# Routed experts on one core: rows without a token skipped, results scattered by GpSimd, spare wide places given to narrow pieces, two preplaced experts

## What the reference computes

```
p_top, g_sel = lax.top_k(p_group, 1)                      # one of 4 groups
e_val, e_sel = lax.top_k(fine, TOP_E)                     # two of its 8 experts
gate = (p_top * jax.nn.softmax(e_val, axis=-1)).reshape(-1)
...
def expert_block(args):
    xb, e = args
    return (jax.nn.silu(xb @ w_gate[e]) * (xb @ w_up[e])) @ w_down[e]
...
out = jnp.zeros((n_tok + 1, d), y_rows.dtype).at[row_token].add(y_rows)[:n_tok]
```

```
layer 0: 21 24 57 58 18 4 1 21 | 1 0 0 0 0 1 0 2 | 25 21 1 22 14 14 28 13 | 96 64 79 163 11 205 0 60
layer 1: 2 82 6 32 15 8 24 9 | 88 35 12 38 24 39 1 47 | 54 193 21 7 48 170 35 28 | 1 0 0 2 1 0 2 0
```

## Time and profile before

| | |
|---|---|
| median of the runs before | 3147.11 us (3146.6 to 3148.13, 3 runs) |
| the profiled execution's own time | 3154.01 us |
| its span in the profile | 3152.0 us |
| TensorE busy | 2810.8 us (89% of the span) |
| VectorE / ScalarE / GpSimd busy | 1619.1 / 679.5 / 410.1 us |
| moved by DMA | 685.03 MB, mean 217 GB/s |

### The profile page before, as it was taken

How to read it: one execution, slowest core, us unless ns; L and a number is a source line. 1 busy time by engine, 2 the same in 40 slices (tenths; PEclk the granted TensorE clock), 3 DMA queues, 4 the chain that set the end, 5 groups by cost and what they waited for, 6 DMA issues and landing times. The chain is left out here.

```text
span 3152.0 us, 36064 instructions
## 1 busy us (share of the span) xinstructions
PE 2810.8 (89%) x13430; PEld 1853.9 (59%) x13430; DVE 1619.1 (51%) x2277; ACT 679.5 (22%) x1202; POOL 410.1 (13%) x257
## 2 busy tenths in 40 slices
PE   9988999999989999969978999785989969999884
PEld 7777888877777887736763333334766743333331
DVE  5575898565567996576971111114667651111112
ACT  1242111022323110073230000003336220000001
POOL 0010113211101113200000000001324000000000
PEclk9998999999989999989989999988999979999897
DMA  5132765233324663164249999995213279999997
GB/s 186 54 141 82 240 207 167 107 120 99 121 93 148 214 218 108 63 185 127 67 157 374 394 392 393 395 405 181 80 53 124 77 264 385 394 391 393 400 395 297
DMA packets 251498, 685.03 MB, mean 217 GB/s; under 512 B 23600, under 2 KB 140316, under 8 KB 197068
## 3 DMA queue, kind: packets, MB, share of 16 engines
q1 hardware_dynamic: 243436, 656.15, 56.7%
q0 software_dynamic: 7904, 26.74, 2.7%
HBM read 628.78 MB, written 54.05 MB: 217 GB/s over the span
## 5 line engine op out<-in xcount | busy, mean ns | idle before, releaser
L2824 PE MATMUL bank<-expert_w_raw,expert_x_turned 128*64 128x512 f32 x2240 | 552.2, 641 | 99.3 <-DMA expert_w_raw<-in_moe_w_up_dram 49.3
L2824 PEld LDWEIGHTS bank<-expert_w_raw,expert_x_turned 128*64 128x64 f32 x2240 | 168.1, 147 | 420.7 <-issue 383.0
L153 PE MATMUL bank<-first_XH,first_w_high 128*128 128x512 f32 (+1 forms) x944 | 370.2, 392 | 0.1
L154 PE MATMUL bank<-first_XL,first_w_high 128*128 128x512 f32 (+1 forms) x944 | 363.4, 385 | 0.0
L155 PE MATMUL bank<-first_XH,first_w_low 128*128 128x512 f32 (+1 forms) x944 | 363.2, 385 | 0.0
L2916 DVE TENSOR_TENSOR expert_hidden<-expert_silu,bank 64x512 f32<-64x512 f32 x70 | 47.5, 679 | 588.0 <-ACT expert_silu L2892 588.0
L233 DVE TENSOR_TENSOR first_w_low<-first_w_raw,first_w_high 128x2048 fp32r<-128x2048 f32 (+2 forms) x94 | 287.1, 3054 | 3.2
L2850 PE MATMUL bank<-expert_w_raw,expert_hidden_turned 128*64 128x512 f32 x1120 | 253.5, 597 | 0.9 <-ACT expert_hidden_turned L2886 0.9
L2775 POOL DMA_INDIRECT expert_x_rows<-h_rows,slot_token x70 | 65.8, 940 | 1126.5 <-PE bank L2800 852.3
L153 PEld LDWEIGHTS bank<-first_XH,first_w_high 128*128 128x128 f32 x944 | 179.7, 190 | 43.9 <-issue 9.8
L154 PEld LDWEIGHTS bank<-first_XL,first_w_high 128*128 128x128 f32 x944 | 179.8, 191 | 37.1 <-issue 2.9
(11 more groups left out here) (550 smaller groups left out, 4665.9 us busy)
## 6 DMA issues: line engine op xcount, KB each, us to landing
expert_w_raw<-in_moe_w_gate_dram SPq DMA_DIRECT2D x120, 1024.0 KB, 17.9
expert_w_raw<-in_moe_w_up_dram SPq DMA_DIRECT2D x120, 1024.0 KB, 20.1
expert_w_raw<-in_moe_w_down_dram SPq DMA_DIRECT2D x120, 1024.0 KB, 20.5
ffn_mod_w<-in_ada_w_dram SPq DMA_DIRECT2D x48, 1024.0 KB, 4.9
first_w_raw<-in_w_up_dram SPq DMA_DIRECT2D x88, 512.0 KB, 6.3
first_w_raw<-in_w_down_dram SPq DMA_DIRECT2D x22, 1024.0 KB, 4.8
first_w_raw<-in_w_in_dram SPq DMA_DIRECT2D x20, 1024.0 KB, 5.0
y_rows<-expert_y SPq DMA_DIRECT2D x140, 128.0 KB, 16.7
```

What stands on the lines that cost most here:

```text
L153: nc.tensor.matmul(out, rounded(st[0]), rounded(mv[0]), start=start, stop=False)
L154: nc.tensor.matmul(out, rounded(st[0]), rounded(mv[1]), start=False, stop=False)
L2824: last = nc.tensor.matmul(out, xT[:, h.parity, kk, :], weights.view(s.parity, 2 * part + w)[:, k, :], start=(kk == 0), stop=(kk == KD - 1))
```

## The change

- `FIRST_EXPERTS` is (0, 16) and no longer 0, 1, 2; each wide place is followed by three narrow ones (`APART` 4); the loop has 15 turns and no longer 17.
- A wide place that no expert needs takes a narrow piece (`at_narrow`, `past_wide`). With the counts above the pattern now makes 28 spans with 33 halves in layer 0 and 30 spans with 35 halves in layer 1, 58 spans and 68 halves in all.
- An empty slot gets an index out of bounds, and the gather skips it; its rows in SBUF keep what they held, so they are zeroed once per phase.
- The result of a half is laid out as 64 rows of 1024 (two products of 64x512 instead of one of 128x512), and GpSimd scatters its rows with an indirect DMA, which skips empty slots too (`slot_row`). SyncE stores nothing any more. The store of span n-2 stands on GpSimd between the gathers of n and of n+1; the last two halves are scattered by `tail_row`.

```diff
-FIRST, WIDE = 3, 5
-NARROW = EXPERTS + (SEQ * TOP_E - EXPERTS) // HALF + 1
+FIRST_EXPERTS, WIDE, APART = (0, 16), 5, 4
+FIRST = len(FIRST_EXPERTS)
+LEAD = WIDE * (APART - 1)
+FIXED = FIRST + WIDE + LEAD
+FURTHER = (EXPERTS + (SEQ * TOP_E - EXPERTS) // HALF + 1 - LEAD) // 2 - 1
+NARROW = LEAD + 2 * FURTHER + 2
...
-LEAD = 2 * WIDE + 2
-FIXED = FIRST + WIDE + LEAD
-FURTHER = (NARROW - LEAD) // 2 - 1
...
+TAIL = 2
+NOWHERE = 16384
...
-        link(V.scalar_tensor_tensor(self.gap, self.narrow_at[:, 0:E], float(HALF), self.gap, ALU.mult, ALU.add))
+        link(V.tensor_scalar(self.at_narrow, self.narrow_at[:, 0:E], self.wide_at[:, E:E + 1], float(WIDE), ALU.add, ALU.subtract))
+        link(V.scalar_tensor_tensor(self.at_narrow, self.at_narrow, 0.0, self.at_narrow, ALU.min, ALU.add))
+        link(V.scalar_tensor_tensor(self.gap, self.at_narrow, float(HALF), self.gap, ALU.mult, ALU.add))
...
-        link(V.tensor_scalar(self.token[0:HALF, :], self.LIST[0:HALF, 0:HALVES], 1.0, 0.0, ALU.subtract, ALU.max))
-        V.tensor_copy(G["slot_token"][0:HALF, :], self.token[0:HALF, :]).then_inc(self.slots_ready, 1)
...
+        link(V.tensor_scalar(self.empty[low, :], listed, 0.5, float(NOWHERE), ALU.is_lt, ALU.mult))
+        link(V.scalar_tensor_tensor(self.token[low, :], self.empty[low, :], -1.0, listed, ALU.add, ALU.add))
+        V.tensor_copy(G["slot_token"][low, :], self.token[low, :]).then_inc(self.slots_ready, 1)
+        push(V.tensor_tensor(self.place_of[low, :], self.empty[low, :], c2["half_row"][low, :], ALU.add))
...
-            def store(s, done=None):
-                for h in s.halves:
-                    sp.wait_ge(y_done, h.at(1))
-                    for c in range(2):
-                        sp.dma_start(G["y_dram"][bass.ds(h.first_row(), HALF), c * BANK:(c + 1) * BANK], y[HALF * c:HALF * c + HALF, h.parity, :]
-                                     ).then_inc(done or stored[h.parity], 16)
...
-                    store(Span(n - 3, j))
...
+            def gather(n):
+                for h in Span(n).halves:
+                    if h.n >= 2:
+                        pool.wait_ge(rows_turned, h.n - 1)
+                    pool.indirect_dma_start(xg[h.parity][:, :], None, G["h_dram"][:, :],
+                                            bass.IndirectOffsetOnAxis(ap=G["slot_token"][0:HALF, h.row:h.row + 1], axis=0),
+                                            bounds_check=SEQ - 1, oob_is_err=False).then_inc(rows_loaded[h.parity], 16)
+
+            def scatter(h, at, done):
+                return pool.indirect_dma_start(G["y_dram"][:, :], bass.IndirectOffsetOnAxis(ap=at, axis=0), y[:, h.parity, :], None,
+                                               bounds_check=BLOCKS * P - 1, oob_is_err=False).then_inc(done, 16)
+
+            def store(n):
+                for h in Span(n).halves:
+                    pool.wait_ge(y_done, 2 * (h.n + 1))
+                    scatter(h, G["slot_row"][0:HALF, h.row:h.row + 1], stored[h.parity])
...
+            for s in range(2):
+                nc.gpsimd.memset(xg[s][:, :], 0.0).then_inc(rows_zeroed, 1)
...
             for n in range(FIXED + 2):
-                for h in Span(n).halves:
-                    gather(h)
+                if n == FIRST:
+                    pool.wait_ge(chain.table_set, 1)
+                gather(n)
+                if n >= TAIL:
+                    store(n - TAIL)
...
-                            dve.wait_ge(stored[h.parity], h.turns(32))
-                        nc.vector.tensor_tensor(y[:, h.parity, :], down_bank(h)[:, :], gain[:, :], ALU.mult).then_inc(y_done, 1)
+                            dve.wait_ge(stored[h.parity], h.turns(16))
+                        for c in range(2):
+                            at = slice(HALF * c, HALF * (c + 1))
+                            nc.vector.tensor_tensor(y[:, h.parity, c * BANK:(c + 1) * BANK], down_bank(h)[at, :], gain[at, :], ALU.mult
+                                                    ).then_inc(last_y_done if last or end else y_done, 1)
```

More of the change, by code:

```diff
@@ L1695, in constant_parts_2 @@
     along = lambda a: np.broadcast_to(np.asarray(a, np.float32), (P, len(a)))
-    own = np.where(np.arange(EXPERTS) < FIRST, HALF, 0)
-    origin = np.where(np.arange(EXPERTS) < FIRST, HALF * np.arange(EXPERTS), 0)
+    own, origin = np.zeros(EXPERTS), np.zeros(EXPERTS)
+    for n, e in enumerate(FIRST_EXPERTS):
+        own[e], origin[e] = HALF, HALF * n
     parts["first_rows"] = along(own)
@@ L2403, in __init__ @@
         self.idx = [now(TT, 1) for _ in range(2)]
-        self.rest, self.n_wide, self.wide_end, self.wide, self.gap_wide, self.second, self.gap, self.n_narrow = [now(EXPERTS) for _ in range(8)]
+        self.rest, self.n_wide, self.wide_end, self.wide, self.gap_wide, self.second, self.gap, self.n_narrow, self.at_narrow, self.ends_narrow = [now(EXPERTS) for _ in range(10)]
         self.wide_at, self.narrow_at = [now(EXPERTS + 1) for _ in range(2)]
@@ L2589, in __init__ @@
         self.parity = n % 2
-        k, place = divmod(n - FIRST, 3)
-        self.wide = FIRST <= n < FIRST + 3 * WIDE and place == 0
+        k, place = divmod(n - FIRST, APART)
+        self.wide = FIRST <= n < FIRST + APART * WIDE and place == 0
         wides = min(max(0, k + (place > 0)), WIDE)
@@ L2762, in _ @@
             for r in range(UP, PLACES):
-                weights.load(sp, r, 1, 1)
-            more = walk(sp, further(sp), step)
-            for n in (FIXED, FIXED + 1):
-                store(Span(n, more), last_stored)
-            sp.wait_ge(last_stored, 64)
+                weights.load(sp, r, 1, second)
+            walk(sp, further(sp), step)
         @block.gpsimd
         def _(pool):
-            def gather(h):
-                if h.n >= 2:
-                    pool.wait_ge(rows_turned, h.n - 1)
-                pool.indirect_dma_start(xg[h.parity][:, :], None, G["h_dram"][:, :],
-                                        bass.IndirectOffsetOnAxis(ap=G["slot_token"][0:HALF, h.row:h.row + 1], axis=0)
-                                        ).then_inc(rows_loaded[h.parity], 16)
@@ L2788, in _ @@
                     for odd in range(2):
-                        gather(Span(FIXED + 2 * pair + odd).halves[0])
+                        gather(FIXED + 2 * pair + odd)
+                        store(FIXED + 2 * pair + odd - TAIL)
+            pool.wait_ge(tail_set, 1)
+            for q in range(TAIL):
+                pool.wait_ge(last_y_done, 2 * (q + 1))
+                scatter(Span(FIXED + q).halves[0], G["tail_row"][0:HALF, q:q + 1], last_stored)
+            pool.wait_ge(last_stored, 32)
         @block.tensor
@@ L2936, in _, with read @@
             dve.wait_ge(gain_set, 2)
-            walk(dve, further(dve), step)
+            def read():
+                more = further(dve)()
+                nc.vector.tensor_copy(G["tail_row"][0:HALF, :], G["slot_row"][0:HALF, bass.ds(Span(FIXED + 2 - TAIL, more).halves[0].at(), TAIL)]
+                                      ).then_inc(tail_set, 1)
+                return more
+            walk(dve, read, step)
 class Combine:
```

61 lines of the change are left out of this document (39 added, 22 removed).

## The result

The changed kernel takes **3294.5 us** (median of 4 runs, 3285.5 to 3303.0) where the kernel before takes 3146.9 beside it (4 runs, 3144.3 to 3148.1): ratio 1.047, 95% interval 1.0441 to 1.0499. It is slower; 3090 was forecast, in a range of 3058 to 3150. The profiled execution took 3285.5 us, its span 3283.6.

What follows compares the result with a forecast made beforehand. DMA was taken to bound the expert phases, TensorE close behind, with groups at 67.5 us. Layer gains of 13.2 and 51.3 less 7.4 took 3154.0 to 3097; the runs' median, 6.9 lower, gave 3090 (range 3058 to 3150).

Steps and rivals of the forecast that it cites:

- Part by part, TensorE: Expert-phase groups: five halves take TensorE 61.3 us, plus 6 us of waits (2.5 to 9.4), 67.3 a group.
- The loop: Expert phases: result, scatter, gather, landing, turning and down matmuls recur, each waiting for the last; 13.4 to 15.3 us.
- the sign named for it: TensorE would wait for gathered rows (`expert_x_rows`) 1 to 3 us in three steps of a group.
- E: The end of span n-2's down matmuls; the gather of span n+1 was put at 2.8 us after it.
- Hidden there: Narrow stretch behind the groups: 13.4 to 15.3 us lie below 16.3 of DMA work, 1 to 3 to spare.
- The DMA part: DMA work in the expert phases: 66.4 and 66.8 us a group; a row gathered and scattered costs 42 ns.
- the lower bound (by bytes): A scattered row's DMA cost priced by bytes like the stores: 10 ns, where the forecast took 17.
- The phase's end: From the last result to the next phase's first transfer: 7.2 us after, 4.2 before, so 3.0 a layer.
- Rival 2: GpSimd's detour decides: indirect DMAs take 2.3 us and not 0.9, groups about 75 us, 3172 us in all; chance 0.09.
- the point of decision: GpSimd's detour decides from 73.2 us a group on, where stalls are 4 us a step.
- Rival 3: Skipped rows free nothing on the DMA engines: a group 73.5 us, a narrow span 17.7, 3164 us in all; chance 0.07.
- Rival 1: DMA alone decides: gathers are in time, rows cost 35 ns, groups 65.4 and 65.7 us, 3068 in all; chance 0.20.

Runs made afterwards that it cites:

- e1: The changed kernel with each gather on GpSimd behind the scatter of span n-3 and no longer n-2: 3082.4 us.
- e2: The changed kernel with gathers behind the scatter of n-3 in the fixed spans (groups) only, n-2 kept in the pairs of narrow spans: 3091.4 us.
- e4: The kernel before, with only its gathers made to skip empty slots; stores, plan and order unchanged: 3095.9 us.
- e7: e1 with no row skipped, in gathers or scatters: 3136.6 us.
- e10: e1 with the last two halves of a phase stored by SyncE and not scattered: 3066.3 us.
- e3: The changed kernel with SyncE storing the results of span n-3 and no scatter; GpSimd only gathers, with skipping: 3070.8 us.
- e5: The changed kernel with 12 more matmuls, all into one half of a bank, ahead of TensorE's wait for rows in narrow steps: 3488.5 us.

## Why the prediction was wrong

**Where the time is.** From the first wide span to the last two spans the prediction had 403.4 and 434.1 us; the profile after has 492.5 (1685.09 to 2177.56) and 529.0 (2684.43 to 3213.46). With 4.0 more at each phase's end that is 192 us, against 188 between the profiled execution and the 3097 forecast for it. Nearly all of it is in the steps of the expert phases.

**The step that failed is "Part by part, TensorE": the loop's price.** The loop was seen: that the gather waits for the scatter of n-2, that this recurs, and the sign named for it came (waits for `expert_x_rows` in three steps a group, though of 3.6 us and not 1 to 3). Its length was not. In the sum of a group its 6 us of waits (2.5 to 9.4) came as 10.8, and the slow work behind them, 10.2 us a group, was put at nothing. By the prediction the loop is 13.4 to 15.3 us; in the step that starts at 1750.21:

| piece | predicted, us | measured, us |
|---|---|---|
| E to the gather's issue | 2.8 | 3.4 (1750.38 to 1753.81; GpSimd started 0.8 after the result, not 0.3) |
| issue to the rows' use | 5.9 to 7.8 | 9.4 (1753.81 to 1763.19) |
| turning, down, up to the next E | 4.7 | 8.3 (1763.19 to 1771.53), two records of the up part among them |
| sum | 13.4 to 15.3 | 21.2 (1750.38 to 1771.53) |

The steps there take 20.8 and 22.4 us (1729.43 to 1750.21 to 1772.56). The first two pieces were short by 0.6 and by 1.6 to 3.5 us. The third was priced at TensorE's full speed, though a stall ahead of it was just what the sum assumed: 8.3 us at a clock of 0.62. At full speed it would be some 5.2 (an estimate: 0.5 for the two records, 1.1 and 3.6), and the loop 18.0 with the measured landing: over the step's length already, and the slow clock adds the other 3. The fall of the clock also makes the stall feed itself, since a slower down gives a later result, a later scatter, a later gather and so the next stall. The slow work is about half the loss: TensorE's busy time is 116.5 us over e1's (2870.2 and 2753.7), its idle time 97 (413.4 and 316.5, span less busy); the waits for rows are 143.4, but e1 for its part waits for weights, 31 us for one matrix's alone. The length of the loop had to be set against the length of the step: 20 us or more, against 16.3 in the narrow stretch and 66.4 / 4 = 16.6 a span in a group.

The Trainium skill has this case: TensorE: Matmul & The Clock Gate (HAM oscillation — how this bites in real kernels) tells of a kernel that waits for data between bursts of matmuls and loses its clock over and over. The trace agrees (1.00, then 0.59 to 0.60, then 1.00 again in the stalled step shown, and down matmuls slower than their 3.65 us a half behind 37 of the 40 waits). The prediction did not weigh it.

**"Hidden there", the narrow stretch.** The wrong side of the same price. It held only in part where the stretch is entered without a stall (e2, 17.0 us a span), and not in the changed kernel (19.6).

**The DMA part held.** With the loop gone (e1) layer 0's groups take 63.3 us and layer 1's narrow spans 15.8, for 66.4 and 16.3. The gathered row was right, 25 ns; the scattered row came out at 11 and not 17, near the lower bound (by bytes), as far as one pair of traces tells. At 36 ns a row the sum has 60 + 767 x 0.036 / 5 = 65.5 us a group; the last three took 64.5, and the first two ran at TensorE's floor.

**The phase's end** was put at 3.0 us a layer over before and is 7.0 (11.2 less 4.2): the scattered tail takes 9.0 us from its issue to the next phase's first transfer (2210.88 to 2219.92), where 5.6 was taken for the landing.

**The rivals.** Rival 2 named the mechanism that decided, at a chance of 0.09, but for a reason that is not there: indirect DMAs are issued in 0.9 us, not 2.3. It set the point of decision at 73.2 us a group; measured are 82.9. Rival 3 falls by e4 and e7: skipped rows do free time. Rival 1, DMA alone (3068), comes near e10 (3066), but that is another kernel, without the loop and with another tail; in the changed kernel the gathers were not in time, and the rival falls by the 40 waits.

## What to carry to other kernels

When an order makes a load wait behind a store of a recent result, write the dependence as a loop and compare its whole length with the step; if it is longer, the step takes the loop's length, whatever each engine's work is. Price what comes behind a stall at the clock that a stall leaves, not at the one of the undisturbed trace. An in-order queue that both loads and stores wants the loads ahead: here one place later for the scatter was worth 212 us, more than the plan and the skipping gathers together (75.3, e3).

## What the runs showed that was not expected

- **Rows skipped by the bounds test** still go through the queue as packets (7904 with and without, e4), and each frees 25 ns in a gather and, by one pair of traces, 11 in a scatter.
- **The fall of the clock is not read from the wait's length alone.** In e2 waits of 2.11 and 2.83 us left the down matmuls behind them at 3.65 us, and one of 2.63 us was followed by 5.44. In the changed kernel one of 2.02 us left them at 3.65, and one of 2.65 was followed by 5.35. What else decides it stays open.
- **Matmuls of 64 columns into the same half of a bank** took 10.03 us for 23 records in e5, 0.44 each; in pairs into both halves they take 3.60 for 16, 0.22 each (the kernel's own).

What makes a gather that follows a scatter take 8.7 us at the median to land (stretch 1725 to 1860 of the changed kernel; 7.7 over the whole run, 7.6 in e1, 7.1 in e3, where no row is scattered) was not settled.
